# A fused decoder step on one Trainium2 core: the down projection as seven block products instead of eight, with the block sums made by GpSimd

## The chip, the core and the metric

The kernel runs on one core of one Trainium2 chip. Such a core has a matrix engine (TensorE, PE in the profile, with its weight loads shown apart as PEld), three engines for elementwise work (VectorE = DVE, ScalarE = ACT, GpSimd = POOL) and SyncE (SP), which here only issues transfers. All have their own instruction streams and meet through semaphores. SBUF is the on-chip memory with 128 partitions, PSUM holds TensorE's results in 8 banks of 128 x 512 floats, DRAM lies outside. The metric is the device time of one launch in microseconds (us), lower is better.

## The reference

The program is one layer of a hybrid decoder: 1024 prompt rows plus 16 meta rows plus 32 rows of 8 running samples (4 each), width 1024. An input projection feeds gated linear attention and latent attention (over the prompt, and over 4096 cached positions for each sample); an output projection, a layer norm, a gated MLP with a causal convolution of width 3, and a second layer norm follow. What the change touches is the last part:

```
a, up = split(h @ w_ffn_in)                  # 2 x 2816 columns
conv  = conv_b + sum(conv_w[j] * ext[:, j:j + T] for j in range(3))
h_out = (silu(conv) * up) @ w_down           # w_down is 2816 x 1024
y     = layer_norm(alpha * h + h_out)        # 1024 prompt rows and 32 sample rows
```

All is float32. The kernel multiplies float32 matrices in three passes on TensorE: each operand is split into a high part, rounded to the engine's fast type (fp32r), and a low part, what is left; high x high, high x low and low x high are added up in PSUM.

## The kernel before

The engines run through the same stages in this order: input projection and linear attention (until about 350 us), latent attention over the prompt (`pe_d`, until about 580), latent attention of the samples over the cache (`pe_e`, until about 775), output projection and norm (`pe_f`), up projection with convolution and gate (`pe_g`, about 905 to 1347), down projection with the last norm (`pe_h`, from 1347).

GpSimd gathers the cached latents by indirect DMAs in `pool_e` (line 1550). The first set of latents and the first rotary block are loaded during prompt attention. The wait `score_done >= N_ATT // 2` (half of the score steps) stands before the second rotary block, and each later set of latents waits for a free slot of three; for set 1 that is the end of all scores. ScalarE's part of sample attention, `act_e` (line 1689), starts when prompt attention's outputs are out (`o_out`) and the latents of the prompt are stored.

The up projection walks over 22 chunks of 128 of the 2816 columns, in loops whose body is one chunk. It is already a Strassen scheme: a chunk has seven products (`product`, line 2215) of 24 matmuls. VectorE sums PSUM banks, makes four block sums of the next chunk's weights (`sums`), two of the three convolution taps and the gate; ScalarE copies, takes the silu and the tap in the middle. A chunk's gated rows are stored by SyncE to `g_res` in DRAM, transposed: 128 rows of the contraction by 32 + 1024 columns (the samples' and the prompt's rows). In the same loops GpSimd does only three small copies in a chunk (`pool_g`, line 2501): `ext<-oldT`, which ScalarE's tap of the chunk waits for, and `newT<-ext` (`keep`).

The down projection (lines 2562 to 2822) reads `g_res` back. Its 66 steps are three groups of prompt row tiles, (1, 2, 3), (4, 5, 6), (7, 8), times 22 blocks k of the contraction. A step loads 128 x 1024 of `w_down` and 128 x 384 (or 256) of `g_res` (`load_d`), ScalarE makes the high parts (`step_high`), VectorE the low parts (`step_low`), and TensorE multiplies: a tile takes two column halves of three matmuls of 128 x 512 each. Raw buffers are 4 deep, split buffers 3 deep. In the second group the samples' 32 rows are multiplied too (`decode`, four small matmuls in a step, straight from the raw buffer), and the kept convolution rows are turned (transposes). A group's sums, statistics and norms are spread by VectorE over the next group's steps; the last two tiles are done at the end, and GpSimd computes the reciprocal deviations and issues most output stores. Loads of steps 2 and 3 are issued while the up projection's last chunk is still multiplying, at its second product (line 2598).

## Time and profile before

| what | value |
|---|---|
| median of 3 runs | 1638.72 us (1634.9 to 1642.35) |
| the profiled execution: own time, span | 1635.87 us, 1634.1 us |
| mean granted clock of TensorE | 0.973 |
| busy: PE, PEld, DVE, ACT, POOL | 94%, 79%, 57%, 41%, 10% |
| from 1347.2 us to TensorE's last matmul | 1347.2 to 1612.4 us |

The span is the time from the first to the last instruction; the execution's own time is 1.8 us longer. "Granted clock" is the share of full speed that the chip's throttle allowed TensorE, 1.00 being 2.4 GHz and 0.50 being 1.2 GHz. Busy PE is read with care, since matmuls are pipelined and overlap in the records: successive starts tell the rate, not the duration of one. "<-" behind a row names what released the engine from its idle time. In the rows below, a time of a single instruction is from its start to its end as recorded, and waiting inside an instruction shows as a longer duration.

### The profile page before, as it was taken

What the parts mean: (1) busy time and instruction counts of PE and PEld (TensorE: products, weight loads), DVE (VectorE), ACT (ScalarE), POOL (GpSimd) and SP (SyncE); (2) the same over time, 40 slices, a digit from 0 to 9 for tenths busy, and PEclk for the clock granted to TensorE, in tenths of its full rate; (3) what the DMA queues carried; (4) which work ended last, traced back from release to release, by engine and by line L of the source; (5) the groups of instructions that cost most, each with busy time, mean ns of one, the idle gap of its engine ahead of it and who ended that gap; (6) DMA issues with size and microseconds to landing.
All of it is one profiled execution on the core that took longest, in us unless ns stands there. A gap on an engine that the chain in (4) does not pass through costs nothing.

```text
span 1634.1 us, 28976 instructions
## 1 busy us (share of the span) xinstructions
PE 1535.8 (94%) x11157; PEld 1287.6 (79%) x11157; DVE 933.1 (57%) x1761; ACT 667.0 (41%) x1283; POOL 165.0 (10%) x265
## 2 busy tenths in 40 slices
PE   6999998799999988798999999999999999999994
PEld 6989997556666655465888999999999998877683
DVE  6624303555455544455568777777777765454495
ACT  2246222633456633234123555555555543332341
POOL 2100000200000024330011000000000000000030
PEclk9999998999899989999999999999999999999997
DMA  7212111110000056654123122222222237645492
GB/s 252 88 54 65 44 53 44 42 52 14 27 1 27 2 219 211 202 184 166 65 90 105 58 75 76 78 78 78 78 78 78 78 110 272 186 148 186 147 302 86
DMA packets 108805, 171.50 MB, mean 105 GB/s; under 512 B 9786, under 2 KB 75192, under 8 KB 108680
## 3 DMA queue, kind: packets, MB, share of 16 engines
q1 hardware_dynamic: 93882, 117.74, 22.8%
q0 software_dynamic: 14688, 52.43, 9.3%
q8 instruction: 63, 1.03, 0.3%
q14 instruction: 28, 0.23, 0.0%
q10 hardware_dynamic: 144, 0.07, 0.0%
HBM read 142.59 MB, written 27.62 MB: 104 GB/s over the span
## 4 chain that ended last, share of the span: by engine, by line
PE 68%; DVE 3%; issue 2%; ACT 1%; another core or an unknown queue 1%; DMA 0%; POOL 0%; SPq 0%; ACTq 0%; DVEq 0%; POOLq 0%
PE ps L2236 9%; PE ps L2235 9%; PE ps L2234 9%; PE ps L210 7%; PE ps L211 7%; PE ps L212 7%; PE ps L1268 4%; PE ps L1598 4%; PE ps L1619 3%; PE ps L1305 2%; PE ps L1645 2%; PE ps L1282 2%; PE ps L2758 1%; DMA f_raw<-in_w_ffn_in 0%
## 5 line engine op out<-in xcount | busy, mean ns | idle before, releaser
L2234 PE MATMUL ps<-t_hi,op_hi 128*128 128x266 f32 (+1 forms) x672 | 191.6, 285 | 2.4 <-DVE gap_hi L2458 2.4
L2236 PE MATMUL ps<-t_hi,op_lo 128*128 128x266 f32 (+1 forms) x672 | 192.2, 286 | 0.0
L2235 PE MATMUL ps<-t_lo,op_hi 128*128 128x266 f32 (+1 forms) x672 | 192.0, 286 | 0.0
L210 PE MATMUL ps<-w_hi,hT_hi 128*128 128x256 f32 (+2 forms) x504 | 142.2, 282 | 3.4 <-DVE hT_lo L324 3.4
L2234 PE MATMUL ps<-h1T_hi,op_hi 128*128 128x266 f32 x504 | 143.4, 285 | 1.0 <-DVE gap_lo L2470 1.0
L2236 PE MATMUL ps<-h1T_hi,op_lo 128*128 128x266 f32 x504 | 144.1, 286 | 0.0
L2235 PE MATMUL ps<-h1T_lo,op_hi 128*128 128x266 f32 x504 | 143.4, 285 | 0.0
L210 PE MATMUL ps<-d_hi,g_hi 128*128 128x512 f32 x352 | 140.8, 400 | 1.2 <-issue 1.2
L212 PE MATMUL ps<-w_hi,hT_lo 128*128 128x256 f32 (+2 forms) x504 | 141.5, 281 | 0.0
L211 PE MATMUL ps<-w_lo,hT_hi 128*128 128x256 f32 (+2 forms) x504 | 141.4, 281 | 0.0
L211 PE MATMUL ps<-d_lo,g_hi 128*128 128x512 f32 x352 | 138.9, 395 | 0.0
L212 PE MATMUL ps<-d_hi,g_lo 128*128 128x512 f32 x352 | 138.7, 394 | 0.0
L2234 PEld LDWEIGHTS ps<-t_hi,op_hi 128*128 128x128 f32 x672 | 126.8, 189 | 2.6 <-DVE gap_hi L2458 2.6
L2235 PEld LDWEIGHTS ps<-t_lo,op_hi 128*128 128x128 f32 x672 | 127.0, 189 | 0.0
L2236 PEld LDWEIGHTS ps<-t_hi,op_lo 128*128 128x128 f32 x672 | 126.6, 188 | 0.0
L210 PEld LDWEIGHTS ps<-w_hi,hT_hi 128*128 128x128 f32 x504 | 97.2, 193 | 3.9 <-DVE hT_lo L324 3.8
L2591 DVE TENSOR_TENSOR g_lo<-g_raw,g_hi 128x384 fp32r<-128x384 f32 (+1 forms) x66 | 33.6, 509 | 113.4 <-ACT d_hi L2585 113.3
L2584 ACT ACTIVATE g_hi<-g_raw 128x384 fp32r<-128x384 f32 (+1 forms) x66 | 32.3, 489 | 160.4 <-PE ps L212 88.3
L212 PEld LDWEIGHTS ps<-w_hi,hT_lo 128*128 128x128 f32 x504 | 97.5, 194 | 0.0
L211 PEld LDWEIGHTS ps<-w_lo,hT_hi 128*128 128x128 f32 x504 | 96.9, 192 | 0.0
L2234 PEld LDWEIGHTS ps<-h1T_hi,op_hi 128*128 128x128 f32 x504 | 95.2, 189 | 1.2 <-issue 1.2
L2235 PEld LDWEIGHTS ps<-h1T_lo,op_hi 128*128 128x128 f32 x504 | 95.0, 189 | 0.0
(351 smaller groups left out, 3473.6 us busy)
## 6 DMA issues: line engine op xcount, KB each, us to landing
d_raw<-in_w_down SPq DMA_DIRECT2D x66, 512.0 KB, 3.6
f_raw<-in_w_ffn_in SPq DMA_DIRECT2D x88, 256.0 KB, 3.4
g_res<-gap_lo SPq DMA_DIRECT2D x22, 528.0 KB, 3.6
g_raw<-g_res SPq DMA_DIRECT2D x44, 192.0 KB, 3.9
w_raw<-in_w_in SPq DMA_DIRECT2D x6, 1024.0 KB, 5.3
xs<-in_x_prompt SPq DMA_DIRECT2D x8, 512.0 KB, 4.5
h_res<-xs POOLq DMA_DIRECT2D x8, 512.0 KB, 3.0
wo_raw<-in_w_o SPq DMA_DIRECT2D x2, 2048.0 KB, 7.5
```

What stands on the lines that cost most here:

```text
L210: nc.tensor.matmul(out, ah, bh, start=start, stop=False)
L211: nc.tensor.matmul(out, ah, bl, start=False, stop=False)
L212: return nc.tensor.matmul(out, al, bh, start=False, stop=stop)
L1268: last = nc.tensor.matmul(ps[:, bank + b, 0:w], qT[0:QD, h, c:c + P], kT[0:QD, h, NS + 512 * b:NS + 512 * b + w], start=True, stop=True)
L1282: last = nc.tensor.transpose(ps[:, 4 + g % 2, P * t:P * t + P], probs[k % 2][:, P * b:P * b + P], ident)
L1305: last = nc.tensor.matmul(ps[VD * e:VD * e + VD, bank, 0:P], v_h[:, b, VD * h:VD * h + VD], ptb[(k - 1 + e) % 3][:, b, :], start=b == 0, s ...
L1598: last = nc.tensor.transpose(ps[:, n % TURN_BANKS, P * j:P * j + P], src, ident)
L1619: last = nc.tensor.matmul(ps[32 * b:32 * b + 32, bank, 0:n], q, x, start=c == 0, stop=c == 2)
L2234: nc.tensor.matmul(o, ah, bh, start=FIRST_IN[q] and k == 0, stop=False, skip_group_check=again)
L2235: nc.tensor.matmul(o, ah, bl, start=False, stop=False, skip_group_check=again)
L2236: last = nc.tensor.matmul(o, al, bh, start=False, stop=k == 3, skip_group_check=again)
L2591: nc.vector.tensor_tensor(g_lo[m % SPL][:, 0:n], g_raw[m % RAW][:, 0:n], g_hi[m % SPL][:, 0:n].bitcast(F32), sub)
```

## The change

The contraction is cut in halves by the parity of the 128-row blocks (even, odd), the prompt rows in two halves of 512 (tiles 1 to 4, 5 to 8) and the output columns in two halves of 512. That gives 2 x 2 block matrices, and the product is formed by seven block products instead of eight (Strassen's scheme in Winograd's form). A block product is 11 steps of 4 tiles of three matmuls, so there are 77 steps with one stationary set of 512 rows and one moving set of 512 columns.

- Block sums of `w_down` (four, `t_res` in DRAM): made by GpSimd in 22 pieces in `pool_e`, eleven before and eleven after the wait for half of the scores (`mix_w`). A piece loads two 128 x 512 blocks by two DMAs, does four 128 x 256 subtractions, each waiting for the one before, and is stored as the next piece begins; from the second piece on, the next load waits for that store. `act_e` now also waits for all 22 stores.
- Block sums of the gated rows (four, `s_res` in DRAM): made by GpSimd after every second chunk of the up projection (`mix_g`): a load of 1 MB, four operations of 128 x 512, a store of 1 MB, and a wait for the store. The eleventh is in `pool_h`.
- The raw loads of steps 0 and 1 wait for the last block sums of the up projection's weights to be read; the loads of steps 2 and on wait for the last product.
- Split buffers are a ring of 11. In the first two products whole rows of `w_down` are loaded, and `decode` runs there. Half of the samples' gated rows (`g_dec[0]`) is loaded after step 3's data and read at the end of step 0.
- The first product is copied out of PSUM by ScalarE after step 13's high part, and the second goes on in the same banks. The third product's third tile waits until VectorE has read the samples' sums (`part_out >= 5`), which stands behind the low part of step 25.
- The last product runs in three passes over the ring: tiles 0 and 1, then 2, then 3. VectorE adds the last product to each tile, takes the rest of the statistics and norms the tiles; all prompt outputs are stored by SyncE at the end.

```diff
+        t_mix = [at(f"t_mix{i}", [P, 4, 256], E0 + 107168 + 4096 * i) for i in range(2)]
+        t_res = nc.dram_tensor("t_res", (FC // 2, P, 4, 512), F32, kind="Internal").ap()
+        mix_loaded = [sem(f"mix_loaded{i}") for i in range(2)]
+        mix_stored = [sem(f"mix_stored{i}") for i in range(2)]
+        T_STORED = 16 * (FC // 2)
+
+        def load_mix(pool, n):
+            j, e = divmod(n, 2)
+            for o in range(2):
+                k = P * (2 * j + o)
+                src = ins["w_down"][k:k + P, :].rearrange("p (c n) -> p c n", c=2)[:, :, 256 * e:256 * e + 256]
+                pool.dma_start(t_mix[e][:, 2 * o:2 * o + 2, :], src).then_inc(mix_loaded[e], 16)
+
+        def store_w(pool, n):
+            j, e = divmod(n, 2)
+            pool.dma_start(t_res[j, :, :, 256 * e:256 * e + 256], t_mix[e][:, :, :]).then_inc(mix_stored[e], 16)
+
+        def mix_w(pool, n):
+
+            j, e = divmod(n, 2)
+            if n == 0:
+                load_mix(pool, 0)
+            else:
+                store_w(pool, n - 1)
+            if n + 1 < FC:
+                if n >= 1:
+                    pool.wait_ge(mix_stored[1 - e], 16 * ((n + 1) // 2))
+                load_mix(pool, n + 1)
+            b11, b12, b21, b22 = [t_mix[e][:, i, :] for i in range(4)]
+            pool.wait_ge(mix_loaded[e], 32 * (j + 1))
+            pool_settle(nc.gpsimd.tensor_tensor(b11, b12, b11, sub))
+            pool_settle(nc.gpsimd.tensor_tensor(b12, b22, b12, sub))
+            pool_settle(nc.gpsimd.tensor_tensor(b22, b22, b11, sub))
+            pool_settle(nc.gpsimd.tensor_tensor(b21, b21, b22, sub))
+
         def pool_e(pool):
             pool.wait_ge(pages_ready, 2)
             slot_free(pool, 0)
             load_latents(0)
             out_of_psum(pool, prep[-1])
             load_rotary(0)
+            for n in range(11):
+                mix_w(pool, n)
             pool.wait_ge(score_done, N_ATT // 2)
...
+            for e in range(2):
+                act.wait_ge(mix_stored[e], T_STORED)
 
...
                 store_gated(sp, c - 1)
-            sp.wait_ge(h1_turned, 2 * NT)
+            sp.wait_ge(op_split, split_count(FC - 1, 5))
             for m in range(2):
                 load_d(sp, m)
...
+        g_mix = at("g_mix", [P, 4, 512], 5440)
+        s_res = nc.dram_tensor("s_res", (FC // 2, P, 4, 512), F32, kind="Internal").ap()
+
+        def mix_g(pool, j):
+
+            pool.wait_ge(g_stored, 32 * j + 32)
+            pool.dma_start(g_mix[:, :, :].rearrange("p (k h) t -> p k (h t)", h=2),
+                           g_res[bass.ds(2 * j, 2), :, NS:NS + SEQ].rearrange("k p t -> p k t")).then_inc(mix_loaded[0], 16)
+            pool.wait_ge(mix_loaded[0], 2 * T_STORED + 16 * j + 16)
+            a11, a21, a12, a22 = [g_mix[:, i, :] for i in range(4)]
+            nc.gpsimd.tensor_tensor(a22, a21, a22, add).then_inc(mix_step, 1)
+            pool.wait_ge(mix_step, 4 * j + 1)
+            nc.gpsimd.tensor_tensor(a21, a11, a21, sub).then_inc(mix_step, 1)
+            pool.wait_ge(mix_step, 4 * j + 2)
+            nc.gpsimd.tensor_tensor(a11, a22, a11, sub).then_inc(mix_step, 1)
+            pool.wait_ge(mix_step, 4 * j + 3)
+            nc.gpsimd.tensor_tensor(a12, a12, a11, sub).then_inc(mix_step, 1)
+            pool.wait_ge(mix_step, 4 * j + 4)
+            pool.dma_start(s_res[bass.ds(j, 1), :, :, :].rearrange("a p c t -> p (a c) t"), g_mix[:, :, :]).then_inc(mix_stored[0], 16)
+            pool.wait_ge(mix_stored[0], T_STORED + 16 * j + 16)
...
+            with pool.Fori(0, FC // 2 - 1) as j:
+                body(2 * j + 1)
+                body(2 * j + 2)
+                mix_g(pool, j)
             body(FC - 1)
...
+        RAW, RING, HALVES = 4, 11, 2
+        NJ = FC // HALVES
+        ring_hi = [at(f"ring_hi{i}", [P, D], E0 + 8192 * i, F32R) for i in range(RING)]
+        ring_lo = [at(f"ring_lo{i}", [P, D], E0 + 8192 * i + 4096, F32R) for i in range(RING)]
...
+        G_LOW, G_HIGH = slice(NS, NS + 512), slice(NS + 512, NS + SEQ)
+        H_PARTS = ((("g", 0, G_LOW), ("w", 0)), (("g", 1, G_LOW), ("w", 1)), (("s", 0), ("t", 3)), (("s", 3), ("t", 0)),
+                   (("s", 1), ("t", 1)), (("s", 2), ("w", 1)), (("g", 1, G_HIGH), ("t", 2)))
+        SET_X, SET_Y = (6, 7, 0, 1), (2, 3, 4, 5)
+        H_BANKS = (SET_X, SET_X, SET_Y, SET_X, SET_Y, SET_X, SET_Y)
+        H_FIRST = (True, False, True, True, False, False, False)
+        DEC_BANK, TURN_BANK = 4, 5
+        N_PARTS = len(H_PARTS)
+        NK = N_PARTS * NJ
...
+        def used(eng, m):
+
+            p, j = divmod(m, NJ)
+            if p < 2:
+                eng.wait_ge(d_used, m + 1)
+            elif j < NJ - 1:
+                eng.wait_ge(d_used, 2 * NJ + (p - 2) * (NJ - 1) + j + 1)
+            else:
+                eng.wait_ge(part_done, 4 * p + 4)
...
         def load_d(sp, m):
...
+            p, j = divmod(m, NJ)
+            a, b = H_PARTS[p]
+            x, done = d_raw[m % RAW], d_loaded[m % RAW]
+            if a[0] == "g":
+                sp.wait_ge(g_stored, 16 * (2 * j + a[1] + 1))
+                src = g_res[2 * j + a[1], :, a[2]]
+            else:
+                sp.wait_ge(mix_stored[0], T_STORED + 16 * (j + 1))
+                src = s_res[j, :, a[1], :]
+            sp.dma_start(x[:, 0:512], src).then_inc(done, 16)
+            if b[0] == "w":
+                k = P * (2 * j + b[1])
+                if p < 2:
+                    sp.dma_start(x[:, 512:1536], ins["w_down"][k:k + P, :]).then_inc(done, 16)
+                else:
+                    sp.dma_start(x[:, 512:1024], ins["w_down"][k:k + P, 512:1024]).then_inc(done, 16)
+            else:
+                sp.wait_ge(mix_stored[0], T_STORED)
+                sp.wait_ge(mix_stored[1], T_STORED)
+                sp.dma_start(x[:, 512:1024], t_res[j, :, b[1], :]).then_inc(done, 16)
...
         def step_high(act, m):
...
             act.wait_ge(d_loaded[m % RAW], 32 * (m // RAW + 1))
...
+            nc.scalar.activation(ring_hi[m % RING][:, :], d_raw[m % RAW][:, 0:1024], ACT.Copy).then_inc(d_high, 1)
...
-            sp.wait_ge(prod_done, product_count(FC - 1, 1))
-            load_d(sp, 2)
-            load_d(sp, 3)
             sp.wait_ge(prod_done, product_count(FC - 1, 6))
...
+            for m in range(2, NK):
+                if m >= RAW:
+                    if m - RAW < 2 * NJ:
+                        used(sp, m - RAW)
+                    else:
+                        sp.wait_ge(d_split, m - RAW + 1)
+                load_d(sp, m)
+                if m == 3:
+                    sp.wait_ge(g_stored, 16 * (FC - 1))
+                    sp.dma_start(g_dec[0][:, :, :], g_res[0:FC:2, :, 0:NS].rearrange("k p t -> p k t")).then_inc(g_dec_loaded[0], 16)
+                if m == 4:
                     store_gated(sp, FC - 1)
...
+                if m == 6:
                     sp.wait_ge(g_stored, 16 * FC)
...
+                    sp.dma_start(g_dec[1][:, :, :], g_res[1:FC:2, :, 0:NS].rearrange("k p t -> p k t")).then_inc(g_dec_loaded[1], 16)
+                    for i in range(2):
+                        sp.wait_ge(h1_stored[i], 16 * (5 - i))
+                if m == 11:
+                    sp.wait_ge(mix_stored[0], T_STORED + 16 * NJ)
+                    sp.dma_start(ydr[:, :], h1_res[0:NS, :]).then_inc(y_loaded[0], 16)
...
+            for t in range(NT - 1):
+                sp.wait_ge(y_ready, t + 2)
+                sp.dma_start(outs["y_prompt"][0, P * t:P * t + P, :], y[t][:, :]).then_inc(y_stored, 16)
...
         def act_h(act):
             for m in range(2, NK):
...
+                if m >= RING:
+                    used(act, m - RING)
+                elif m == 2:
+                    act.wait_ge(prod_done, product_count(FC - 1, 3))
+                elif m == 3:
                     act.wait_ge(prod_done, product_count(FC - 1, 5))
...
+                elif m == 4:
+                    act.wait_ge(prod_done, product_count(FC - 1, 6))
                 step_high(act, m)
...
+                if m == NJ + 2:
+                    for t in range(4):
+                        act.wait_ge(part_done, t + 1)
+                        nc.scalar.activation(hp1[:, t, :], ps[:, SET_X[t], :], ACT.Copy).then_inc(parts_kept, 1)
+                j = m - 6
...
+            def decode_sum():
+                dve.wait_ge(d_used, 2 * NJ)
+                dve.wait_ge(y_loaded[0], 16 * 5)
                 for q in range(4):
                     last = nc.vector.tensor_copy(yd[:, 256 * q:256 * q + 256], ps[NS * q:NS * q + NS, DEC_BANK, 0:256])
...
+                last.then_inc(part_out, 1)
+                dve.wait_ge(part_out, 5)
...
                 step_low(dve, m)
                 if m == 2:
                     gated_up(dve, FC - 1)
-                if not g:
-                    continue
-                n = FIRST_SUM[g] - FIRST_SUM[g - 1]
-                if k == 1:
-                    group_sums(g - 1)
+                if m == 24:
+                    dve.wait_ge(y_loaded[0], 16 * 5)
+                    for t in range(4):
+                        c11(t)
+                if m == 25:
...
+            for t in range(NT - 1):
+                g, u = divmod(t, 4)
+                cols = HIGH if g == 0 else LOW
+                dve.wait_ge(y_step, (0, 8)[g] + u + 1)
+                dve_settle(nc.vector.tensor_tensor(y[t][:, cols], y[t][:, cols], take(5 + g, u), add))
+                last_stats(t, 1 - g)
+                if t in (1, 2, 3):
+                    norm(t, P, y[t - 1][:, :])
+                if t >= 3:
+                    norm(t + 1, P, y[t][:, :])
...
+            def part(m, t):
+                p, j = divmod(m, NJ)
+                b = ps[:, H_BANKS[p][t], :]
+                hi, lo = ring_hi[m % RING], ring_lo[m % RING]
+                again = not H_FIRST[p]
+                ah, al, bh, bl = hi[:, P * t:P * t + P], lo[:, P * t:P * t + P], hi[:, 512:1024], lo[:, 512:1024]
+                if j == 0:
+                    free(p, t)
+                nc.tensor.matmul(b, ah, bh, start=j == 0 and not again, stop=False, skip_group_check=again)
+                nc.tensor.matmul(b, ah, bl, start=False, stop=False, skip_group_check=again)
+                last = nc.tensor.matmul(b, al, bh, start=False, stop=j == NJ - 1, skip_group_check=again)
+                if j == NJ - 1:
+                    last.then_inc(part_done, 1)
                 return last
 
+            def free(p, t):
+                if p == 0 and t < 2:
+                    pe.wait_ge(old_out, 1)
+                elif p == 0:
+                    pe.wait_ge(x_out, ext_count(FC - 1))
+                elif p == 1:
+                    pe.wait_ge(parts_kept, 6 + t + 1)
+                elif p == 2 and t < 2:
+                    pe.wait_ge(acc_out, acc_count(FC - 1, C21))
+                elif p == 2 and t == 2:
+                    pe.wait_ge(part_out, 5)
+                elif p == 2:
+                    pe.wait_ge(parts_kept, 6)
+                else:
+                    pe.wait_ge(part_out, out_count(p - 3, t))
+
...
+                p, j = divmod(m, NJ)
+                if j == 0:
+                    pe.wait_ge(g_dec_loaded[p], 16)
+                if m == 0:
+                    pe.wait_ge(acc_out, acc_count(FC - 1, C12))
...
+                    last = nc.tensor.matmul(ps[NS * q:NS * q + NS, DEC_BANK, 0:256], g_dec[p][:, j, :],
+                                            d_raw[m % RAW][:, 512 + 256 * q:768 + 256 * q], start=m == 0, stop=m == 2 * NJ - 1)
...
+                for t in range(4):
+                    last = part(m, t)
+                if p < 2:
                     last = decode(m)
...
+            for pairs in ((0, 1), (2,), (3,)):
+                for m in range(NK - NJ, NK):
                     pe.wait_ge(d_split, m + 1)
-                    last = tile(m, t)
-                last.then_inc(tile_done, 1)
+                    for t in pairs:
+                        part(m, t)
...
+            mix_g(pool, NJ - 1)
+            pool.wait_ge(parts_kept, 6)
```

`d_raw` holds 128 x 1536 floats: the stationary rows first, the moving columns behind. Between steps VectorE also adds the parts: after the low part of step 24 the first four tiles' left halves (`c11`), after 25 `decode_sum`, after 36 `u2_out`, after 47 `c22_part`, after 58 `u3_out`, and single sums and statistics after steps 48 to 66.

## Rows read from the trace of the kernel before

**Rows 1.** chain that ended last, shares of the span by line (page, part 4)
```profile
PE ps L2236 9%; PE ps L2235 9%; PE ps L2234 9%; PE ps L210 7%; PE ps L211 7%; PE ps L212 7%; PE ps L1268 4%; PE ps L1598 4%; PE ps L1619 3%; PE ps L1305 2%; PE ps L1645 2%; PE ps L1282 2%; PE ps L2758 1%; DMA f_raw<-in_w_ffn_in 0%
```

**Rows 2.** window of the down projection: busy time (instructions), granted clock, DMA share, GB/s
```profile
1347.20:1443.50 96.30, 96.30 (x417) 77.67 (x415) 46.79 (x58) 34.33 (x46) 0.00 (x0) 1.00 0.60 202
```

**Rows 3.** timeline of ScalarE in the second third of the down projection: start, us, idle before
```profile
1500.49 0.52 ACT L2584 ACTIVATE g_hi<-g_raw 128x384 fp32r<-128x384 f32 x1 [3.49 <-PE ps L2758]
1500.93 1.04 ACT L2585 ACTIVATE d_hi<-d_raw 128x1024 fp32r<-128x1024 f32 x1
1505.46 0.53 ACT L2584 ACTIVATE g_hi<-g_raw 128x384 fp32r<-128x384 f32 x1 [3.50 <-PE ps L2758]
```

**Rows 4.** timeline of SyncE there: start, us
```profile
1500.86 0.43 SPq L2575 DMA_DIRECT2D g_raw<-g_res  x1
```

**Rows 5.** timeline of GpSimd during attention
```profile
417.18 0.94 POOL L1532 DMA_INDIRECT ring_r<-in_cache_krope,rope_at  x1 [0.30 <-issue]
...
501.45 0.95 POOL L1532 DMA_INDIRECT ring_r<-in_cache_krope,rope_at  x1 [0.30 <-issue]
572.33 0.94 POOL L1525 DMA_INDIRECT ring_c<-in_cache_ckv,row_at  x1 [69.93 <-PE ps L1268]
```

**Rows 6.** GpSimd by line and shape: busy, mean ns | idle before
```profile
L436 POOL DMA_DIRECT2D h_res<-xs x9 | 5.7, 629 | 3.5 <-DVE xs L314 3.5
...
L426 POOL MEMSET v_t<- 128x512 f32 x1 | 0.5, 525 | 0.1
```

**Rows 7.** DMA issues: KB each, median us from issue to landing
```profile
d_raw<-in_w_down SPq DMA_DIRECT2D x66, 512.0 KB, 3.6
...
h_res<-xs POOLq DMA_DIRECT2D x8, 512.0 KB, 3.0
...
out_ckv_prompt<-zt POOLq DMA_DIRECT2D x1, 1024.0 KB, 5.2
...
g_dec<-g_res SPq DMA_DIRECT2D x1, 352.0 KB, 5.7
```

**Rows 8.** timeline of ScalarE where sample attention begins
```profile
586.04 0.29 ACT L1706 ACTIVATE sprob<-ps,sst_m 128x32 f32<-128x32 f32 x1 [2.05 <-DVE sst_m L1784]
```

**Rows 9.** windows there; columns as in rows 2
```profile
580.00:584.00 4.00, 0.40 (x4) 0.00 (x0) 0.00 (x0) 0.28 (x1) 1.67 (x2) 0.50 1.02 403
584.00:588.00 4.00, 3.46 (x37) 3.37 (x38) 2.02 (x7) 0.98 (x3) 0.00 (x0) 0.50 1.04 394
```

**Rows 10.** timeline of GpSimd, late in the down projection
```profile
1557.37 2.95 POOL L307 TENSOR_SCALAR stat<-stat 32x1 f32<-32x1 f32 x1 [50.53 <-DVE stat L302]
```

**Rows 11.** timeline of VectorE there
```profile
1557.49 1.20 DVE L2592 TENSOR_TENSOR d_lo<-d_raw,d_hi 128x1024 fp32r<-128x1024 f32 x1
...
1560.15 1.21 DVE L2592 TENSOR_TENSOR d_lo<-d_raw,d_hi 128x1024 fp32r<-128x1024 f32 x1
```

**Rows 12.** timeline of VectorE in one chunk of the up projection
```profile
1173.53 0.78 DVE L2466 TENSOR_TENSOR gap_hi<-ps,gap_hi 128x266 f32<-128x266 f32 x2 [0.92 <-PE ps L2236]
1174.33 0.77 DVE L2470 TENSOR_TENSOR gap_lo<-ps,gap_hi 128x266 f32<-128x266 f32 x2
```

**Rows 13.** timeline of ScalarE there
```profile
1176.46 0.20 ACT L2335 ACTIVATE ext<-ps 128x32 f32<-128x32 f32 x1 [2.23 <-PE ps L2236]
...
1180.52 1.28 ACT L2273 ACTIVATE conv<-ext,vcol 128x1072 f32<-128x1072 f32 x1 [0.49 <-DVE ext L2483]
```

**Rows 14.** timeline of GpSimd there
```profile
1160.29 0.18 POOL L2512 COPY newT<-ext 128x2 f32 x1
```

**Rows 15.** timeline of ScalarE, a copy out of PSUM
```profile
1445.71 0.57 ACT L2650 ACTIVATE new_rows<-ps 18x512 f32<-18x512 f32 x1
```

**Rows 16.** timeline of VectorE at the end
```profile
1617.28 0.67 DVE L2658 SCALAR_TENSOR_TENSOR y<-y,ps 128x512 f32<-128x512 f32 x1
...
1621.24 1.28 DVE L314 SCALAR_TENSOR_TENSOR y<-y,stat,ln2b 128x1024 f32<-128x1024 f32 x1
```

**Rows 17.** timeline of TensorE at the end
```profile
1612.01 0.40 PE L212 MATMUL ps<-d_hi,g_lo 128*128 128x512 f32 x1
```

328 lines of the change are left out of this document (110 added, 218 removed).

## The prediction

> **What bounds the kernel.** I read the chain of waits first: TensorE's lines hold most of it, and the down projection's three lines (L210 to L212, shared with other three-pass products) are 7% each [rows 1]. So matmuls taken out of that stage come off the end, unless a wait takes their place. The windows of the stage show it: in 96.3 us TensorE is never idle, its clock is granted in full (1.00, the 2.4 GHz level), while VectorE and ScalarE are busy for half or less and the DMAs for 0.60 [rows 2]. That window is 23 steps of 18 matmuls, 414 in all (the count holds three of the stage before), so one takes 96.3 / 414 = 0.2326 us. Then I read who is idle beside it. GpSimd issues a few gathers during attention and otherwise waits; its free stretches are 418.1 to 497.7 and 502.4 to 572.3 [rows 5]. The whole question is whether the sums fit in them, and which waits the new order of the down projection brings.
>
> **Removed matmuls.** Before: 22 blocks x 8 tiles x 2 halves x 3 = 1056. After: 77 steps x 4 tiles x 3 = 924. 132 x 0.2326 = 30.7 us less, all on the path. The samples' small matmuls stay: a step without transposes takes 4.97 us [rows 3], 18 x 0.2326 = 4.19 of it, so `decode` is 0.78. The first 22 steps are then 12 x 0.2326 + 0.78 = 3.57 us, later ones 2.79. Casts keep up: 1.04 us on ScalarE [rows 3] and 1.20 on VectorE [rows 11] in a step. Traffic per step is 768 KB in 3.57 us (215 GB/s) and 512 KB in 2.79 (184 GB/s), about the 202 GB/s at which the stage runs now [rows 2].
>
> **Waits added in the down projection.** Three stand where buffers pass from one use to the next.
> - `g_dec[0]` before the first `decode`. SyncE must issue four loads (0.43 each [rows 4], 1.8 with hand-overs) after the last product, then this one. The whole of `g_dec` lands after 5.7 us; half of it between 3.6 (the large loads) and 5.7 [rows 7], I take 5.0. TensorE is there after 12 x 0.2326 = 2.8: a wait of 1.8 + 5.0 + 0.1 - 2.8 = 4.1 (2.7 to 4.8). The late loads of steps 2 and 3 land in its shadow.
> - The copy of product 1. ScalarE does it behind the high part of step 13, whose load waits for step 9's `decode`. From there: issue and landing 4.5 [rows 4, 7], cast 1.04, copy 0.57 [rows 15], together 6.2 with hand-overs. TensorE has only step 10 to do, 3.57: a wait of 2.7.
> - `part_out >= 5` at step 22. From the end of step 20: the load of step 24 (4.0, it is smaller), cast 1.04, low part 1.2, four sums of 0.67 [rows 16], low part of step 25 1.2, four small copies at about 0.3 (1.2): 11.3 us. TensorE has step 21 and two tiles, 3.57 + 1.40 = 4.97: a wait of 6.4. VectorE stands in order, so nothing passes this.
> Together 13.2 us; with loads faster or slower by 0.5, 11 to 15. In sample attention an idle stretch is followed by work at the lower clock: 0.50 (1.2 GHz) for at least 4 us [rows 9], so 2 us can be lost each time. Three shorter waits: I add 3 (0 to 6).
>
> **The end.** After the last matmul of before (1612.4 [rows 17]) VectorE takes until 1622.5 [rows 16], 10.1 us. In the changed order a tile costs it 1.65 (a sum of 0.67, half the statistics about as long, their joining at 0.25) and a norm of 2.6 (twice 1.28) [rows 16]. The first four tiles take 4 x 1.65 + 4 x 2.6 = 17.0, the others 4 x (1.65 + 2.6 + 1.0 for GpSimd's part) = 21.0, and all stands behind the low part of step 76 (2.4): 40.4 from the start of the last product, which takes TensorE 132 x 0.2326 = 30.7. So 9.7 behind it: -0.4 us.
>
> **GpSimd's 22 pieces during attention.** This is the largest unknown. A piece (after the first) is a serial loop: the store of the piece before must land, two loads are issued, four operations follow one another.
> - Store, 512 KB: the same size on the same queue took 3.0 (rows of 4 KB); 1 MB in pieces of 1 KB took 5.2 [rows 7]. These pieces are of 1 KB: 3.3 with the hand-over (3.1 to 5.2).
> - Two load issues: 0.63 for a plain DMA [rows 6] to 0.94 for a gather [rows 5] each; I take 0.7, 1.4 in all.
> - Four operations of 128 x 256: no row has a GpSimd operation of this kind. A memset of 128 x 512 takes 0.525 [rows 6], 0.26 per 256 columns of one stream, and the fixed part shows in the copy of two columns, 0.18 [rows 14]. One stream is the floor (0.3), three streams one after the other the ceiling (0.26 x 3 + 0.18 = 1.0). I take two reads in turn, 0.65, and 0.1 to hand over: 4 x 0.75 = 3.0.
> So a piece is 7.7 us. The Trainium skill (GPSIMD Engine Reference, Performance versus the Vector engine) gives 4497 ns for such an operation at 2048 columns; estimated down to 256 that is about 0.6, and by it a piece would be 7.5; no run here shows it.
> The last store lands at 418.1 + 6.3 (first piece) + 21 x 7.7 + 5.0 (rotary gathers) + 3.3 = 594.4. ScalarE's first instruction of sample attention is at 586.0 now [rows 8] and would wait for it; the sums run 22 us over the free stretch, but latents of set 1 are needed only some 8 us after ScalarE starts, and their gathers are issued while the last store lands. Added: 8.4 us. The bounds of its parts: at 7.2 us a piece nothing is added, at 9.1 (operations of 1.0) 38, and each 0.1 us in a piece is 2.1 us of the launch. That is why this term makes the range.
>
> **GpSimd's sums in the up projection.** `mix_g` starts when `newT<-ext` is done, K = 1160.5 [rows 14]. Load of 1 MB 4.7 (from 3.0 and 5.2 [rows 7]), four operations of 128 x 512 (2 x 0.53 + 0.18, with hand-over 1.3 each) 5.2, store 5.0: free at K + 15, and queued behind it is only the copy that ScalarE's tap waits for at 1180.5, K + 20 [rows 13]. 5 us are left, and a late tap has some 4 more before a product waits. VectorE is the other half: in this stretch it works nearly without a gap on operations with two inputs in SBUF. The trace shows who gives way: a GpSimd operation on one column lasted 2.95 us while VectorE's such operations went by at their usual 1.20 and 1.21 [rows 10, 11]. So GpSimd's sums stretch, up to 5 us, and VectorE hardly does. I take 1 us (0 to 3) over the ten pairs of chunks. The last sums, in the down projection, are due before step 12 is loaded, some 30 us after its start; they need about 26.
>
> **Sum.** -30.7 + 13.2 + 3 - 0.4 + 8.4 + 1 = -5.5 us. On the profiled execution's 1635.87 (span 1634.1 and 1.8 around it) that is 1630.4; the median of the runs lies 2.85 above, so 1633.2. I say 1633. A kernel like this can be told from no change at about 0.5%, 8.2 us, so the forecast lies inside that.
>
> **Rivals.**
> - The pieces fit. If a piece takes 7.2 us or less (operations of 0.5 and a store of 3.1 would do), attention loses nothing: -13.9, 1624.8; with smaller down-projection waits to 1616. For it: GpSimd's 3.0 us stores. Against: four operations in series that no row prices.
> - The pieces overrun, slower. From 8.0 us a piece on (an operation of 0.72, or a store of 3.6) the overrun eats the whole gain; at 8.8 the last store lands at 617.5, 31.5 late, and the sum is +17.5: 1656. TensorE would stand idle before sample attention as it does at 580 [rows 9], only longer. For it: 1 KB pieces and a store that nothing overlaps.
> - VectorE is held in the up projection. If a running GpSimd operation held VectorE for its 1.2 us, the four would push VectorE back by some 3.4 us in that stretch; it has 0.92 of idle before the sum after product 3 [rows 12], and that pair of sums must end (1175.1) before product 5 starts (1176.4 [rows 13]), another 1.3. 1.2 us of wait remain ten times, more where all four collide: +12, and the sum is +5.5: 1644. [Rows 10, 11] show the other direction only. The Trainium skill (SBUF — State Buffer, SBUF: two separate sides) states the pair of ports as an exclusive lock that whoever starts first keeps for the whole instruction; by that rule this rival is what happens. The trace agrees in that one blocks the other entirely, but its only case has GpSimd passed over by one VectorE operation after another.
> - The block products don't save their share, because a matmul in the new order costs more than 0.2326. Same shapes, same three passes, same clock speak against it; I give it nothing.
>
> **Chances.** Forecast (pieces of 7.3 to 8.0) 0.40, of which 0.16 with smaller waits than taken, beyond -8.2; pieces fit 0.28; overrun 0.20; VectorE held 0.12. Faster by over 0.5%: 0.16 + 0.26 = 0.42. Slower by over 0.5%: 0.16 of the overrun and 0.06 of the held VectorE and 0.03 of the rest, 0.25. Within: 0.33. Range: from 1615 (fit, small waits) to 1656 (a piece of 8.8); the forecast's own range is 1623 to 1641.
>
> **What would show it.** Right: 924 matmuls at 0.233 us in the last stage; TensorE waits of about 4, 3 and 6 us at the first `decode`, at step 11 and at step 22; ScalarE's first sample-attention operation at about 594 with `mix_stored` behind it; the period of the up projection's chunks unchanged. Wrong: a GpSimd subtraction of 128 x 256 clearly off 0.65 or a store off 3.3 (then the first or second rival decides), two long chunks in every pair (the third), or loads in the first 22 steps that land later than 7 us after their issue, since TensorE would then wait in each of those steps, which would make all of this too low.

## The result, and the profile after

| | median | ratio to before, 95% interval | span of the profiled execution |
|---|---|---|---|
| before | 1640.53 us (1634.9 to 1645.55) | | 1634.1 us |
| after | 1677.61 us (1675.27 to 1680.05) | 1.0227 (1.0187 to 1.0268) | 1673.8 us |

The changed kernel is 2.3% slower; 1633 was forecast, and 1677.6 lies above the range's end of 1656. The first thing to read is where the 39.7 us of span are. (The medians lie 37.1 us apart; the kept traces are of runs shorter than the medians.) The timeline, asked for the matmuls that read one tile, gives a row with count, shortest, median and longest duration in ns, and the first and last start. Three such rows cut the launch into stages: `hr` starts the output projection, `t_hi` the up projection, and the last row (whose two matmuls per tile share a form) the down projection. Before:

```profile
L2026 PE MATMUL ps<-consts,hr x72: 222/272/273, 797.5 to 890.5; 128*128 128x128 f32 x64, 48*128 48x48 f32 x8
...
L2234 PE MATMUL ps<-t_hi,op_hi x672: 279/284/389, 912.9 to 1346.9; 128*128 128x266 f32 x84, 128*128 128x264 f32 x84
...
L210 PE MATMUL ps<-d_hi,g_hi x352: 387/394/504, 1347.3 to 1611.5; 128*128 128x512 f32 x176
```

After:

```profile
L2070 PE MATMUL ps<-consts,hr x72: 221/272/273, 831.1 to 924.0; 128*128 128x128 f32 x64, 48*128 48x48 f32 x8
...
L2278 PE MATMUL ps<-t_hi,op_hi x672: 279/284/395, 946.3 to 1393.8; 128*128 128x266 f32 x84, 128*128 128x264 f32 x84
...
L2844 PE MATMUL ps<-ring_hi x308: 387/389/796, 1394.2 to 1648.8; 128*128 128x512 f32 x154
```

All that lies ahead of the output projection is 33.6 us longer (831.1 against 797.5). The up projection, from its first matmul to the next stage's, takes 447.9 us where it took 434.4: +13.5. The down projection, from first to last row, takes 254.6 where it took 264.2: -9.6. What follows it takes 25.0 where it took 22.6: +2.4. The output projection itself, from its first row to the up projection's, is 0.2 us shorter (115.2 against 115.4). Sum +39.7.

The chain of waits tells the first of these at a glance. Matmuls were nearly all of it [rows 1]; now a transfer's name stands among them (page, part 4):

```profile
PE ps L2278 6%; PE ps L2280 6%; PE ps L2279 6%; DMA t_res<-t_mix 4%; PE ps L2844 3%; PE ps L2845 3%; PE ps L2846 3%; PE ps L1638 2%; PE ps L210 2%; PE ps L211 2%; PE ps L212 2%; DMA f_raw<-in_w_ffn_in 2%; PE ps L1659 2%; POOL t_mix L1561 2%; PE ps L1685 1%
```

It is ScalarE that waits for it, with its first instruction of sample attention; this row answers to [rows 8], where it stood at 586.04:

```profile
615.70 0.29 ACT L1748 ACTIVATE sprob<-ps,sst_m 128x32 f32<-128x32 f32 x1 [35.33 <-DMA t_res<-t_mix]
```

What it waits for is GpSimd's work in attention. One piece of the 22, in GpSimd's timeline, is the work between two stores:

```profile
434.70 0.76 POOL L1565 DMA_DIRECT2D t_res<-t_mix  x1 [0.30 <-POOL t_mix L1583]
438.36 1.43 POOL L1561 DMA_DIRECT2D t_mix<-in_w_down  x2 [2.90 <-DMA t_res<-t_mix]
439.81 0.73 POOL L1580 TENSOR_TENSOR t_mix<-t_mix 128x256 f32<-128x256 f32 x1
...
442.23 0.73 POOL L1583 TENSOR_TENSOR t_mix<-t_mix 128x256 f32<-128x256 f32 x1
443.25 0.76 POOL L1565 DMA_DIRECT2D t_res<-t_mix  x1 [0.30 <-POOL t_mix L1583]
```

8.55 us: 3.66 for the store and the wait for its landing, 1.45 for two load issues, 3.44 for four operations with their hand-overs. 7.7 was forecast, as 3.3, 1.4 and 3.0.

In the up projection, VectorE and GpSimd side by side. VectorE first (the 128x1072 operation takes 1.33 alone, the sums 0.69 each):

```profile
993.76 2.36 DVE L2422 SCALAR_TENSOR_TENSOR conv<-ext,vcol,conv 128x1072 f32<-128x1072 f32 x1
...
996.73 1.10 DVE L2444 TENSOR_TENSOR s_sum<-f_raw,f_raw 128x512 f32<-128x512 f32 x1
997.87 1.67 DVE L2444 TENSOR_TENSOR s_sum<-s_sum,f_raw 128x512 f32<-128x512 f32 x1
999.46 1.78 DVE L2444 TENSOR_TENSOR s_sum<-f_raw 128x512 f32<-128x512 f32 x1
```

GpSimd in the same 7 us (alone, in the down projection, such an operation takes 1.27 to 1.29):

```profile
993.36 1.64 POOL L2555 TENSOR_TENSOR g_mix<-g_mix 128x512 f32<-128x512 f32 x1 [4.66 <-DMA g_mix<-g_res]
995.07 2.21 POOL L2557 TENSOR_TENSOR g_mix<-g_mix 128x512 f32<-128x512 f32 x1
997.36 1.63 POOL L2559 TENSOR_TENSOR g_mix<-g_mix 128x512 f32<-128x512 f32 x1
999.07 1.62 POOL L2561 TENSOR_TENSOR g_mix<-g_mix 128x512 f32<-128x512 f32 x1
```

Both sides stretch; neither gives way alone. The ends (start plus duration) come in turn: GpSimd 995.00, VectorE 996.12, GpSimd 997.28, VectorE 997.83, GpSimd 998.99, VectorE 999.54, GpSimd 1000.69, each a little less than one undisturbed operation behind the other side's. TensorE then waits for what VectorE does next; over the whole launch its waits for `gap_lo` grew from 1.0 us to 10.7, which is 9.7 of the 13.5 (page, part 5, before and after):

```profile
L2234 PE MATMUL ps<-h1T_hi,op_hi 128*128 128x266 f32 x504 | 143.4, 285 | 1.0 <-DVE gap_lo L2470 1.0
...
L2278 PE MATMUL ps<-h1T_hi,op_hi 128*128 128x266 f32 x504 | 144.1, 286 | 10.7 <-DVE gap_lo L2514 10.7
```

In the down projection its waits are (from 1390 us on; us in total, times, longest):

```profile
PE ps L2844 <- DVE yd L2768: 8.9, 1, 8.9
PE ps L2874 <- DMA g_dec<-g_res: 5.0, 1, 5.0
PE ps L2844 <- ACT h_part L2729: 3.8, 1, 3.8
PE ps L2894 <- ACT new_rows L2734: 1.8, 1, 1.8
```

The windows of this stage (columns as in [rows 2]) show the clock behind them, which was 1.00 throughout before:

```profile
1394.00:1416.00 22.00, 17.03 (x85) 11.19 (x84) 9.63 (x12) 6.03 (x6) 0.70 (x1) 0.84 0.72 225
1416.00:1440.00 24.00, 22.20 (x137) 15.33 (x134) 7.79 (x6) 9.12 (x12) 5.70 (x5) 1.00 0.82 267
1440.00:1452.00 12.00, 8.22 (x41) 5.59 (x40) 3.90 (x4) 5.12 (x7) 1.05 (x2) 0.88 0.68 231
...
1487.00:1500.00 13.00, 4.07 (x20) 2.43 (x20) 8.25 (x12) 4.84 (x5) 0.00 (x0) 0.75 0.87 299
```

These stretches hold the waits as well. Cut finer, the clock stood at 0.50 when TensorE had gone back to work, after each of the three longest waits:

```profile
1404.00:1406.00 2.00, 2.00 (x6) 1.54 (x6) 0.00 (x0) 0.00 (x0) 0.00 (x0) 0.50 0.90 219
1450.00:1452.00 2.00, 2.00 (x6) 1.58 (x5) 0.93 (x1) 1.03 (x1) 0.00 (x0) 0.50 0.00 0
1500.00:1502.00 2.00, 2.00 (x6) 1.61 (x5) 1.93 (x5) 1.09 (x2) 0.19 (x1) 0.50 0.18 69
```

There the matmuls start 0.43 us apart (1500.43, 1500.86) where they start 0.23 apart at 1.00.

### The profile page after: what moved, and what is told of

It reads as the page before. It is cut to its first block, busy times and chain, and to the rows that moved or that the text cites. A ratio compares the mean times of both kernels' runs of the same rounds, so it can differ in the third digit from the quotient of the medians.

```text
span 1673.8 us, 29093 instructions
## 1 busy us (share of the span) xinstructions
PE 1513.3 (90%) x11025; PEld 1265.5 (76%) x11025; DVE 966.9 (58%) x1733; ACT 655.2 (39%) x1232; POOL 366.2 (22%) x479
## 3 DMA queue, kind: packets, MB, share of 16 engines
q1 hardware_dynamic: 97930, 120.89, 22.6%
## 4 chain that ended last, share of the span: by engine, by line
PE 40%; DVE 9%; DMA 9%; issue 7%; POOL 7%; ACT 2%; another core or an unknown queue 1%; SPq 1%; DVEq 0%; ACTq 0%; POOLq 0%
PE ps L2278 6%; PE ps L2280 6%; PE ps L2279 6%; DMA t_res<-t_mix 4%; PE ps L2844 3%; PE ps L2845 3%; PE ps L2846 3%; PE ps L1638 2%; PE ps L210 2%; PE ps L211 2%; PE ps L212 2%; DMA f_raw<-in_w_ffn_in 2%; PE ps L1659 2%; POOL t_mix L1561 2%; PE ps L1685 1%
## 5 line engine op out<-in xcount | busy, mean ns | idle before, releaser
L2278 PE MATMUL ps<-h1T_hi,op_hi 128*128 128x266 f32 x504 | 144.1, 286 | 10.7 <-DVE gap_lo L2514 10.7
L2674 DVE TENSOR_TENSOR ring_lo<-d_raw,ring_hi 128x1024 fp32r<-128x1024 f32 x77 | 94.5, 1234 | 84.7 <-ACT ring_hi L2670 84.2
L2670 ACT ACTIVATE ring_hi<-d_raw 128x1024 fp32r<-128x1024 f32 x77 | 81.7, 1061 | 143.5 <-DMA d_raw<-in_w_down 76.1
L2844 PE MATMUL ps<-ring_hi 128*128 128x512 f32 x308 | 125.0, 406 | 12.7 <-DVE yd L2768 8.9
L2845 PE MATMUL ps<-ring_lo,ring_hi 128*128 128x512 f32 x308 | 122.5, 398 | 0.0
L2846 PE MATMUL ps<-ring_hi,ring_lo 128*128 128x512 f32 x308 | 122.1, 397 | 0.0
L1638 PE MATMUL ps<-consts,ring_c 128*128 128x128 f32 x512 | 69.1, 283 | 47.7 <-ACT pastT L1736 38.6
L1638 PEld LDWEIGHTS ps<-consts,ring_c 128*128 128x128 f32 x512 | 57.1, 144 | 66.8 <-ACT pastT L1736 42.9
```

Source lines behind the costliest of these rows:

```text
L1638: last = nc.tensor.transpose(ps[:, n % TURN_BANKS, P * j:P * j + P], src, ident)
L2278: nc.tensor.matmul(o, ah, bh, start=FIRST_IN[q] and k == 0, stop=False, skip_group_check=again)
L2670: nc.scalar.activation(ring_hi[m % RING][:, :], d_raw[m % RAW][:, 0:1024], ACT.Copy).then_inc(d_high, 1)
L2674: nc.vector.tensor_tensor(ring_lo[m % RING][:, :], d_raw[m % RAW][:, 0:1024], ring_hi[m % RING][:, :].bitcast(F32), sub).then_inc(d_split, 1)
L2844: nc.tensor.matmul(b, ah, bh, start=j == 0 and not again, stop=False, skip_group_check=again)
L2845: nc.tensor.matmul(b, ah, bl, start=False, stop=False, skip_group_check=again)
```

## The experiments

All stage times below are read as above, from the first starts of the three groups. "To start" is the output projection's first transpose, "up" and "down" the two projections. They are from one kept trace of each kernel. Each ratio is to runs of the kernel before taken alongside (their medians are 1637.94 to 1641.86 us), so it is not the quotient of the medians listed. e1, e2, e3, e7 and e9 leave out sums that `y` needs: they show what the sums cost, and are no kernels to use.

| kernel | median us | ratio to before (95%) | to start | up | down | span |
|---|---|---|---|---|---|---|
| before | 1640.53 | | 797.5 | 434.4 | 264.2 | 1634.1 |
| after | 1677.61 | 1.0227 (1.0187 to 1.0268) | 831.1 | 447.9 | 254.6 | 1673.8 |
| e1, no sums of w_down | 1643.05 | 1.0033 (1.0016 to 1.0050) | 802.8 | 447.8 | 255.3 | 1642.2 |
| e2, no gated sums | 1660.69 | 1.0133 (1.0104 to 1.0162) | 832.6 | 434.5 | 255.2 | 1660.2 |
| e3, neither | 1629.58 | 0.9947 (0.9930 to 0.9964) | 798.9 | 434.4 | 254.8 | 1626.1 |
| e4, loads behind the operations | 1660.76 | 1.0143 (1.0119 to 1.0166) | 813.8 | 447.8 | 254.6 | 1656.0 |
| e5, wide pieces | 1651.01 | 1.0082 (1.0064 to 1.0099) | 804.6 | 447.6 | 254.5 | 1646.6 |
| e6, early load of gated rows | 1664.68 | 1.0161 (1.0144 to 1.0178) | 831.2 | 437.5 | 255.0 | 1663.5 |
| e7, memsets for the gated sums | 1662.64 | 1.0148 (1.0122 to 1.0173) | 830.3 | 434.5 | 257.1 | 1661.0 |
| e8, three edits, down projection | 1653.83 | 1.0094 (1.0075 to 1.0114) | 831.2 | 447.8 | 234.3 | 1653.0 |
| e9, wide pieces, memsets | 1647.18 | 1.0032 (1.0018 to 1.0045) | 804.9 | 447.7 | 254.8 | 1646.9 |
| e10, first of e8's edits | 1669.21 | 1.0162 (1.0138 to 1.0185) | 834.6 | 448.0 | 247.9 | 1669.8 |
| e11, combined | 1622.55 | 0.9888 (0.9868 to 0.9907) | 808.4 | 437.4 | 234.2 | 1619.6 |

The theory was that three costs lie in three stages and add up: pieces that overrun attention (some 30 us), GpSimd and VectorE in each other's way in the up projection (13.5), and three waits with the clock behind them in the down projection. The rivals were traffic, an attention late for another reason, and waits that come back under another name.

### e1 to e3: taking the sums away

```diff
# e1
-            for n in range(11):
-                mix_w(pool, n)
...
-                sp.dma_start(x[:, 512:1024], t_res[j, :, b[1], :]).then_inc(done, 16)
+                sp.dma_start(x[:, 512:1024], ins["w_down"][k:k + P, 512:1024]).then_inc(done, 16)
# e2
                 body(2 * j + 2)
-                mix_g(pool, j)
...
-                src = s_res[j, :, a[1], :]
+                src = g_res[2 * j + a[1] % 2, :, G_LOW if a[1] < 2 else G_HIGH]
# e3: both
```

> Leaves out: the block sums of w_down (GpSimd's 22 pieces in attention, their loads and stores, and ScalarE's wait for them); the down projection reads unsummed blocks of w_down in their place, in transfers of the same shape.
> Theory A (the pieces overrun the attention; ScalarE's first instruction of the sample attention came 29.7 us and the first transposes of the output projection 33.5 us later than before): that instruction returns to about 586 us, and the whole is 30 to 34 us shorter than the changed kernel, about 1645.
> Rival B (attention would have ended late anyway, by the product's other parts: more traffic or ScalarE's new copies): at most 10 us shorter, 1668.
> Rival C (the pieces' loads and stores also slow the prompt's attention and the rest before 586 us): more than 36 us shorter, 1638 or less.

> Leaves out: the block sums of the gated rows (GpSimd's work, its load and its store in every second turn of the up projection's loop); the down projection reads unsummed rows of the same size in their place. The sums of w_down stay.
> Theory A (GpSimd's four 128x512 operations and VectorE's hold each other up in the up projection; the stretch from 946.2 to 1394.1 us is 13.5 us longer than before's): that stretch goes back to about 434 us, the whole is 13 us shorter, about 1664.
> Rival B (the loop turned by two bodies, or other traffic, costs it): the stretch stays over 444 us, the whole within 3 us of the changed kernel.
> The down projection should stay at 255 us, with the same three waits.

> Leaves out both: the block sums of w_down and those of the gated rows. What is left of the change is seven products with their copies and sums in place of eight.
> Theory A (the two costs are independent and nothing else is late): 30 to 34 and 13 us together, about 1631, which is 9 to 10 us below the kernel before: all that seven products give as they are placed here.
> Rival B (the costs overlap, one hides a part of the other): 1637 or more.
> Rival C (the down projection's own waits come from late sums or from the sums' traffic): they shrink from 19.5 us in all, and the time falls below 1622.

Theory A held in all three. Without the pieces ScalarE's first instruction of sample attention is back at 585.13 us, and the ratio falls by 0.0194, 32 us. Without the gated sums the up projection takes 434.5 us, as before. In e3 both are gone: 1626.1 against 1673.8, 47.7 us of span, where e1 and e2 alone gave 31.6 and 13.6, 45.2 in all; by the ratios it is 0.0280 against 0.0194 + 0.0094 = 0.0288. So the two costs add up. The down projection stays at 255 us in all three, with its waits (9.5, 5.0 and 4.9 us in e3): they come from neither the sums nor their traffic, and e3's rival C falls. What seven products are worth, so placed and with their sums left out, is 0.5%.

One remainder: in e1, 217.7 us pass between ScalarE's first instruction and the output projection, in e3 214.7, before 211.5, with no piece near them. That is the part of the 33.6 us which the 29.7 of the late start leave. What takes these 3 to 6 us was not found. It is 213.5 to 217.8 us in all twelve kernels with the seven products, with and without pieces, and each figure is from one execution; the runs of the kernel before spread over 10.7 us (1634.9 to 1645.55), so it may be scatter in part.

### e4 and e5: what a piece costs

```diff
# e4: mix_w
-            if n + 1 < FC:
-                if n >= 1:
-                    pool.wait_ge(mix_stored[1 - e], 16 * ((n + 1) // 2))
-                load_mix(pool, n + 1)
...
             pool_settle(nc.gpsimd.tensor_tensor(b21, b21, b22, sub))
+            if 1 <= n < FC - 1:
+                pool.wait_ge(mix_stored[1 - e], 16 * ((n + 1) // 2))
+                load_mix(pool, n + 1)
# e5: one buffer of 128 x 4 x 512, 11 pieces
+        t_mix = at("t_mix", [P, 4, 512], E0 + 107168)
...
+            load_mix(pool, j, 0)
+            load_mix(pool, j, 1)
...
+            pool.wait_ge(mix_loaded[0], 16 * (j + 1))
             pool_settle(nc.gpsimd.tensor_tensor(b11, b12, b11, sub))
+            pool.wait_ge(mix_loaded[1], 16 * (j + 1))
             pool_settle(nc.gpsimd.tensor_tensor(b12, b22, b12, sub))
+            store_w(pool, j, 0)
             pool_settle(nc.gpsimd.tensor_tensor(b22, b22, b11, sub))
             pool_settle(nc.gpsimd.tensor_tensor(b21, b21, b22, sub))
+            store_w(pool, j, 1)
```

> Complete. In each of GpSimd's pieces, the wait for the last store and the next piece's loads are moved behind the piece's four operations, so that the store runs while the operations do.
> Theory A (a piece of 8.53 us is a sum of parts in series: 0.76 issue of the store, about 3 waiting for it, 2 x 0.72 issue of the loads, 4 x 0.81 for the operations): the wait of 3 us shrinks by the 3.2 us of the operations unless the loads' own landing (3 us) becomes the wait; the loads' landing is then no longer covered by operations but by the other piece's store issue and operations. About 6.0 to 7.3 us a piece, the first instruction of the sample attention at 586 to 592 us, the whole 22 to 30 us shorter, about 1650.
> Rival B (the transfers themselves are the limit, slowed by the attention's own traffic): 8 us or more a piece, less than 10 us gained.

> Complete. GpSimd sums w_down in 11 pieces of 4 blocks of 128x512 in one buffer (its two halves loaded and stored apart) in place of 22 of 4 blocks of 128x256 in two buffers; 8 pieces before the second rotary load, 3 after. The buffers take the same room.
> Theory A (a piece is a series of waits and issues, whatever its size; seen in the reordered pieces: 8.0 us with 2.5 us of waiting for loads left, where 2.9 us of waiting for stores had been): per 4x512, issues 2 x 0.72 + 2 x 0.76, waits of 2 to 3 us, four operations at 1.3 us (the gated sums' undisturbed time): 10 to 11 us, 11 of them 110 to 121 us, plus the rotary load; done at about 540 us, and ScalarE's first instruction of the sample attention is back at 585 to 586. The whole is 30 to 34 us shorter than the changed kernel, about 1644, as when the sums of w_down are left out.
> Rival B (the time goes by bytes: 4x512 takes twice 8.5 us): the last store lands after 600 us and nothing is gained.

e4 fell between its theories. The wait for the store is gone from GpSimd's timeline; a wait for the loads stands in its place:

```profile
445.35 0.77 POOL L1565 DMA_DIRECT2D t_res<-t_mix  x1
448.47 0.72 POOL L1577 TENSOR_TENSOR t_mix<-t_mix 128x256 f32<-128x256 f32 x1 [2.34 <-DMA t_mix<-in_w_down]
...
451.90 1.45 POOL L1561 DMA_DIRECT2D t_mix<-in_w_down  x2 [0.30 <-POOL t_mix L1580]
453.35 0.77 POOL L1565 DMA_DIRECT2D t_res<-t_mix  x1
```

8.0 us a piece instead of 8.55, and ScalarE starts at 598.49. With two buffers, a load and a store of over 3 us each must both land in the round of one buffer, and only one can hide behind the other buffer's operations. The order chooses which. That is my reading of the two timelines; no run takes one of the transfers away.

In e5 a piece of twice the size takes 13.1 us in the mean of ten, the rotary gathers taken out (the first 13.5: successive first operations at 423.33 and 436.81), not the 10 to 11 expected: a load of 512 KB lands after 4.9 us in the median. Against 17.1 for two of the old ones it is enough: ScalarE starts at 591.1, and the ratio falls by 0.0145. But 586 was expected, and nothing of the pieces stands in the way at 591: the last store was issued at 566.7, and ScalarE waits for the same operation of VectorE's as before (`sst_m`, 2.0 us).

### e9: what else the pieces cost in attention

```diff
# on e5, four times
-            pool_settle(nc.gpsimd.tensor_tensor(b11, b12, b11, sub))
+            pool_settle(nc.gpsimd.memset(b11, 0.0))
```

> Leaves out the arithmetic of the sums of w_down: the wide pieces with a 128x512 memset in the place of each of the 44 operations (0.5 us in place of 1.27); their loads, stores and order stay. What it is for: with the wide pieces, ScalarE's first instruction of the sample attention came at 591.1 us, not at 586, with nothing of the pieces in its way; VectorE's copies rs<-rinv (128x128, 32 of them) took 419 ns there and 227 before, and TensorE waited for them 6.1 us in place of 1.8.
> Theory A (GpSimd's reading operations hold up those copies of VectorE's, and by them the prompt's attention): the copies are back at 227 ns and the first instruction at 585 to 586; the whole 4 to 6 us shorter than with the wide pieces, about 1646.
> Rival B (the pieces' transfers take the 5 us): the instruction stays at 590 or later.

First what led to it. VectorE's groups by shape in attention, before:

```profile
L1417 DVE COPY rs<-rinv 128x128 f32<-128x128 f32 x32 | 7.3, 227 | 1.2
```

and with the wide pieces (e5), where its larger groups that read or write PSUM keep their means within 4 ns:

```profile
L1417 DVE COPY rs<-rinv 128x128 f32<-128x128 f32 x32 | 13.4, 419 | 1.2
```

One such copy of e5, and GpSimd beside it:

```profile
466.50 1.63 DVE L1417 COPY rs<-rinv 128x128 f32<-128x128 f32 x1
```

```profile
466.75 1.29 POOL L1575 TENSOR_TENSOR t_mix<-t_mix 128x512 f32<-128x512 f32 x1
```

The copy lasts until the operation beside it ends (468.13 and 468.04). Four of the 32 copies took 1.1 us or more, each beside such an operation; copies beside the issue of a piece's transfer alone took their 0.23.

With memsets the copies took 277 ns in the mean and ScalarE started at 588.79: between the theories. What A meant to do with memsets did not work: a memset holds the copy up as well, only for its own 0.5 us. One of e9:

```profile
467.39 0.86 DVE L1417 COPY rs<-rinv 128x128 f32<-128x128 f32 x1
```

```profile
467.63 0.54 POOL L1575 MEMSET t_mix<- 128x512 f32 x1
```

Shorter operations gave back 2.3 of the 5.1 us; 2.8 remain, of which the copies' remaining excess (32 x 0.05) is 1.6 at most. Whether transfers take the rest stays open. In the kept traces the 2.3 us don't reach the output projection (it starts at 804.9, in e5 at 804.6), while the ratio is 0.0050 lower than e5's, some 8 us (5 to 12 by the intervals) where 4 to 6 were expected; so what the held copies cost the launch is not settled.

### e6 and e7: the gated sums

```diff
# e6: in the loop's second body
                 nc.gpsimd.tensor_copy(e[:, :, 0:2], oldT[...]).then_inc(ext_old, 1)
+                if j is not None:
+                    load_g(pool, j)
                 keep(c)
# e7: four times
-            nc.gpsimd.tensor_tensor(a22, a21, a22, add).then_inc(mix_step, 1)
+            nc.gpsimd.tensor_tensor(a22[:, 0:8], a21[:, 0:8], a22[:, 0:8], add)
+            nc.gpsimd.memset(a22[:, 8:512], 0.0)
+            nc.gpsimd.memset(a12[:, 8:512], 0.0).then_inc(mix_step, 1)
```

> Complete. In the up projection, GpSimd issues the load of the gated rows before it copies the second product's last rows (keep), in place of after it, so that the four operations begin about 4 us earlier within the loop's turn and GpSimd is free again earlier.
> Theory A (what costs is that GpSimd's operations run beside VectorE's own and each holds the other up, wherever they lie): VectorE's work is dense all through the turn, and the gain is under 4 us of the 17 us which leaving the sums out gave.
> Rival B (what costs is only where they lie: beside the subtraction whose end TensorE waits for): 8 us or more gained, about 1667.

> Leaves out the gated sums' arithmetic: in the place of each of the four 128x512 additions of GpSimd stand an addition of 8 columns and two memsets of 504 columns; load, store and the order stay. The results are not the sums.
> Theory A (GpSimd's reading operations and VectorE's share a way into SBUF, and an operation that only writes doesn't take it): VectorE's 512-column operation beside them goes back from 2.36 us to 1.33, the waits for gap_lo in the up projection from 10.7 us to about 1, and the whole to that without the gated sums, 13 to 17 us shorter than the changed kernel, about 1662.
> Rival B (any operation of GpSimd's holds VectorE up): VectorE is held up for as long as the memsets last, and the gain is less than 7 us.
> Rival C (the transfers of the gated sums cost it, not the operations): no gain.

e7: theory A. With the transfers in place and the reading operations gone, the up projection takes 434.5 us, as without any sums; rivals B and C fall. VectorE's group, after and then in e7:

```profile
L2422 DVE SCALAR_TENSOR_TENSOR conv<-ext,vcol,conv 128x1072 f32<-128x1072 f32 x42 | 65.0, 1548 | 0.0
```

```profile
L2422 DVE SCALAR_TENSOR_TENSOR conv<-ext,vcol,conv 128x1072 f32<-128x1072 f32 x44 | 58.4, 1327 | 0.0
```

e6: rival B. The same four sums, 4 us earlier, cost 3.1 us in the up projection, not 13.5. VectorE's work is held up no less than before; it is only other work. In e6:

```profile
L2403 DVE TENSOR_TENSOR op_lo<-f_raw,op_hi 128x512 fp32r<-128x512 f32 x61 | 61.0, 1002 | 28.1 <-ACT op_hi L2305 27.8
```

These take 692 ns in e2 and e7, with 45 us of idle time before them; here the idle time pays. After the change, the held operations stood between TensorE's product and the sum it waits for.

### e8 and e10: the waits of the down projection

```diff
# e10 (and e8): VectorE
+                if m == 23:
+                    decode_out()
                 if m == 24:
...
-                    pe.wait_ge(part_out, 5)
+                    pe.wait_ge(part_out, 1)
# e8 besides
-                if m == NJ + 2:
+                if m == NJ + 1:
...
             store_gated(sp, FC - 2)
+            sp.wait_ge(g_stored, 16 * (FC - 1))
+            sp.dma_start(g_dec[0][:, :, :], g_res[0:FC:2, :, 0:NS].rearrange("k p t -> p k t")).then_inc(g_dec_loaded[0], 16)
```

> Complete. Three edits in the down projection alone: VectorE's copy of the samples' sums out of PSUM comes ahead of its work of step 24 and of the four sums of product 2, and frees TensorE's bank by itself (the wait of 8.9 us); ScalarE's copy of product 1 comes one step earlier (3.8 us); the samples' first gated rows are loaded before the last product of the up projection (5.0 us).
> Theory A (each wait is a late releaser and TensorE's time is lost there): they shrink by 8, 2.7 and 4 us, and the whole is about 14 us shorter than the changed kernel, 1663.
> Rival B (VectorE or the loads are the pace behind them, so the waits come back under another name): less than 6 us.

> Complete. Of the three edits in the down projection only the first: the copy of the samples' sums out of PSUM ahead of VectorE's work of step 24, with a count of its own.
> Theory A (the three waits add up, and each gives what it shows, with the clock that falls behind the longest of them, 0.75 in the stretch 1487 to 1500): of the 20.3 us by which the down projection was shorter with all three, this one gives 8.9 and some 2 us of clock, about 11; the stretch of the down projection is 243 to 244 us, the whole about 1665.
> Rival B (the clock's part is larger, and most of the 20 us hangs on this wait): 15 us or more.

e8 gave 20.3 us in the down projection, more than its 14. TensorE's waits there, by the same view as above:

```profile
PE ps L2897 <- ACT new_rows L2733: 3.6, 2, 1.9
PE ps L2847 <- DVE ring_lo L2676: 0.7, 1, 0.7
PE ps L2847 <- ACT h_part L2728: 0.3, 1, 0.3
PE ps L2847 <- DVE yd L2767: 0.2, 1, 0.2
```

4.8 in place of 19.5: 14.7 us. That leaves 5.6 by subtraction, and the windows show where: cut in these four stretches the clock was 0.95, 0.92, 0.96 and 0.75 after the change, and is 1.00 in all of e8's.

```profile
1394.00:1402.00 8.00, 8.00 (x48) 5.49 (x47) 5.53 (x9) 3.37 (x4) 0.00 (x0) 1.00 0.80 276
1402.00:1440.00 38.00, 34.16 (x206) 22.89 (x205) 13.40 (x11) 14.72 (x20) 8.34 (x8) 1.00 0.83 281
1440.00:1487.00 47.00, 46.66 (x254) 31.56 (x253) 20.54 (x22) 14.65 (x15) 0.00 (x0) 1.00 0.80 270
1487.00:1500.00 13.00, 12.26 (x54) 9.80 (x53) 10.86 (x12) 5.59 (x6) 5.69 (x3) 1.00 0.79 263
```

e10 missed below: 6.7 us, where 11 was expected for the removed wait of 8.9; rival B, 15 or more, falls. The wait is gone (0.2 is left), and the clock of 0.75 behind it too (1.00 from 1491 on). But 13.6 us of waits remain. The copy of product 1 is waited for 5.4 us in place of 3.8 and `new_rows` 2.4 in place of 1.8; these two waits end at 1454 and 1426 us, ahead of the edited place, so the edit did not make them longer. The same wait for product 1's copy took 3.8 to 5.5 us in the other kernels that have the down projection as it is (5.5 in e2). Without these 2.2 us the gain would have been 8.9, what the wait shows; the 2 us of clock expected on top are not seen. (`ring_lo`, 0.6 us at 1507, is new, in e8 too.) Before 1491 the clock is 0.93, about what it is after the change over the same stretches. The other two edits of e8 were not run alone.

### e11: combined

Its edits are those of e5, e6 and e8.

> Complete. Wide pieces, early load of the gated rows, and the three edits in the down projection together.
> Theory A (the costs lie in different stages and add up): output projection from 804.6 us (as with the wide pieces), up projection 437.5 us (early load), down projection 234.3 us (three edits), 24.5 us behind the last product: span 1617, in the runs' terms about 1619, 1.2% below the kernel before.
> Rival B (the down projection's gain shrinks since the gated sums or the loads are late for it, or the clock falls elsewhere): 1625 or more.

Theory A, with a span of 1619.6 for 1617 and a median of 1622.6 for 1619: up projection and down projection 437.4 and 234.2 us as expected, only the start at 808.4 in place of 804.6 (in sample attention; ScalarE's first instruction is at 590.65, as in e5). The median is 1622.55 us, 1.1% below the kernel before and 3.3% below the changed one.

## Why the prediction was wrong

- **Removed matmuls, -30.7: right in kind, too small.** In e8 the down projection is 29.9 us shorter than before with 4.8 us of waits still in it: -34.7. The count is as forecast (308 rows of each of three lines, 924), but the price was not. The prediction took 0.2326 us a matmul for the new order too; where nothing waits and `decode` is over, they start 123.8 / (182 x 3) = 0.2267 us apart, in e8:

```profile
L2848 PE MATMUL ps<-ring_lo,ring_hi x183: 389/389/389, 1505.0 to 1628.8; 128*128 128x512 f32 x183
```

  Over the last 55 steps (660 matmuls) that is 3.9 us. Why the new order is quicker is not shown. The last rival asked whether a matmul would cost more than 0.2326, and nothing asked whether it would cost less.
- **Waits in the down projection, 13.2 and 3 for the clock: right in kind, too small.** 5.0, 3.8 and 8.9 were measured for 4.1, 2.7 and 6.4, plus 1.8 for `new_rows`, not foreseen: 19.5. The clock took 5.6 for 3, near the 2 us for each wait that the prediction had read from [rows 9]. Together 25.1 against 16.2; with the matmuls' -34.7 that makes the measured -9.6.
- **The end, -0.4:** +2.4. It took 25.0 after the change, 20.9 (e1) to 24.6 in the other kernels, 22.6 before; a small miss.
- **GpSimd's 22 pieces, +8.4: the step that failed first.** The term gave the piece 7.7 us; its average was 8.63 ((612.15 - 426.17 - 4.8 for the rotary gathers) / 21). Two parts were short: the store (it lands 3.4 us after its issue begins, with the hand-over 3.66 for 3.3), and the operation (0.727 for 0.65, with hand-overs 3.44 for 3.0). The first piece took 8.3 us, not 6.3. 21 x 0.93 + 2.0 = 21.5, and ScalarE started at 615.7, not at 594.4: 29.7 us late instead of 8.4, and e1, without the pieces, gives them back. The mechanism and its slope (2.1 us per 0.1) stood in the text, as did the rival with 8.8 us a piece and 31.5 late. The two sizes measured, 0.727 at 256 columns and 1.27 at 512, differ by 0.54 for 256 columns and leave 0.19 as the fixed part. The Trainium skill's figure (GPSIMD Engine Reference, Performance versus the Vector engine), 4497 ns at 2048 columns, lies on that line (0.19 + 8 x 0.54 = 4.5); it had been scaled down without a fixed part, so 0.6 came out.
- **GpSimd's sums in the up projection, +1: the second failure, +13.5.** The step said "VectorE hardly does" stretch, from one operation on one column that VectorE passed over [rows 10, 11]. That row shows the case in which VectorE's operations follow one another without a gap and GpSimd's comes second. With GpSimd's operations in a row as well, each side is blocked in turn. The third rival named this, at +12, and got a chance of 0.12. Its reason is the rule of the Trainium skill (SBUF — State Buffer, SBUF: two separate sides). In my words: VectorE's operations with two inputs in SBUF contend for a port pair only with GpSimd operations that read SBUF, its operations in a performance mode that uses both ports with any of GpSimd's, and one operation keeps the pair to its end. The traces agree: the two-input operation takes 1.55 us in the mean beside sums and 1.33 beside memsets, the copies `rs<-rinv` are held by both, and the groups on PSUM of the up projection by neither (`gap_lo<-ps,gap_hi` 435 ns after the change and in e7). That these copies run in such a mode no row shows. One held copy's recorded start (466.50) lies ahead of that of the operation that holds it (466.75), so recorded starts don't tell who has the pair.

With these two terms alone at their measured sizes the sum is -30.7 + 13.2 + 3 - 0.4 + 29.7 + 13.5 = +28.3. The prediction had both in its rivals (31.5 late, and +12) but weighed them as alternatives; both came true at once, which no chance and no end of its range allowed for. With every term as measured it is -34.7 + 25.1 + 2.4 + 33.6 + 13.5 - 0.2 = +39.7, the difference of the spans; of the 33.6, some 3.9 are the part that no run explains.

## What to carry to other kernels

Price a chain of transfers and operations from issue to issue, every link; where its slack is used up, a miss of 0.9 us a piece comes 21 times, and here one larger piece was worth more than a better order of two small ones. A sum moved to GpSimd is not beside VectorE's two-input operations but in turn with them: put it where VectorE has idle time ahead of what TensorE awaits. In TensorE's own stage, count for a wait its length and then the clock. And rivals that lie in different stages can come true together: add them up before setting the end of the range.

## What the runs showed of the hardware

- A copy of VectorE's within SBUF, 0.23 us alone, lasted up to 1.70 us beside GpSimd's 128x512 subtraction (e5), and up to 0.86 us beside its memset (e9); VectorE's 128x1072 operation with two inputs was not held up by memsets (1327 ns, e7), only by sums (1548 ns in the mean, single ones 2.36 us, after the change). I had expected a memset to hold up nothing.
- After waits of 5.0, 3.8 and 8.9 us in the down projection, TensorE's granted clock stood at 0.50, the 1.2 GHz level, and matmuls of 128x512 started 0.43 us apart; with no wait over 1.9 us (e8) it stayed at 1.00, the 2.4 GHz level. By subtraction that was worth 5.6 us, over a third of the waits' own 14.7.
- The same three-pass matmuls of 128x512 started 0.2326 us apart in the order of before and 0.2267 us apart in the new order, both at a granted clock of 1.00.
- GpSimd's issue of a 512 KB store took 0.76 us in rows of 1 KB (after the change) and 0.58 in rows of 4 KB (e5).
